# The gates' columns on the first v pair, four-tile o slots, and the rows' chain spread over the last group, in a hybrid mLSTM/conv decoder layer

## The reference, cut to what matters

```python
h_in = rms_norm(x, pre_mix_norm_w)
proj = h_in @ w_in            # q, k (1024) | v (512) | o (512) | gates (8) | conv value (512) | conv gate (512)
qk = silu(causal_depthwise_conv(qk_raw, qk_conv_w) + qk_conv_b)          # width 4
gates = gates + gate_bias; i_pre, f_pre = gates[:, :4], gates[:, 4:]
h = mlstm_chunkwise(q, k, v, i_pre, f_pre)    # chunks of 128; per chunk and head: cumulative log
                                              # forget gate, running maximum, decays, carried state
y_mlstm = sigmoid(o_pre) * layer_norm(h) * w
u = conv_val * sigmoid(conv_gate); u = causal_depthwise_conv(u, conv_w)  # width 31
y_conv = silu(layer_norm(u))
x = x + rms_norm(concat(y_mlstm, y_conv) @ w_out)
x = x + rms_norm(square(relu(rms_norm(x) @ w_ff1)) @ w_ff2)
```

## Time and profile before

| | us |
|---|---|
| three runs | 2145.79, 2147.93, 2150.26; median 2147.93 |
| the profiled execution | 2149.32 |
| its span | 2147.5 |
| TensorE busy | 2090.3 |
| VectorE busy | 1441.8 |
| ScalarE busy | 903.3 |
| GpSimd busy | 416.3 |

### The profile page before, as it was taken

The page is one execution under the profiler, slowest core; times in us unless marked ns, Lnnn a source line. Parts: engine busy times, 40 slices in busy tenths (PEclk is TensorE's granted clock), DMA queues, the critical chain, the costliest instruction groups (busy, mean ns, idle before and its releaser), DMA issues. The chain is left out here.

```text
span 2147.5 us, 27070 instructions
## 1 busy us (share of the span) xinstructions
PE 2090.3 (97%) x10177; PEld 1752.4 (82%) x10177; DVE 1441.8 (67%) x1965; ACT 903.3 (42%) x1512; POOL 416.3 (19%) x254
## 2 busy tenths in 40 slices
PE   7999999999979999999999999999999999999998
PEld 5897878888978888778888778888888888888886
DVE  6797999889157777776666866666654536534276
ACT  5532434234344544655544644455423313313153
POOL 0000000000010231243332332233172144400012
PEclk9999999999999999999999999999999999999999
DMA  5021212112174686664455655544875454443375
GB/s 198 25 89 47 67 40 84 55 40 81 55 271 154 223 270 222 210 199 141 139 159 181 227 161 162 162 147 125 280 253 222 142 230 172 175 176 138 137 253 207
DMA packets 253520, 339.18 MB, mean 158 GB/s; under 512 B 11536, under 2 KB 196112, under 8 KB 239568
## 3 DMA queue, kind: packets, MB, share of 16 engines
q1 hardware_dynamic: 219344, 316.29, 43.9%
q10 hardware_dynamic: 33728, 21.04, 3.1%
q0 software_dynamic: 320, 0.13, 0.0%
HBM read 226.14 MB, written 111.28 MB: 157 GB/s over the span
## 5 line engine op out<-in xcount | busy, mean ns | idle before, releaser
L1651 PE MATMUL psum<-x_hi,w_hi_P 128*128 128x512 f32 x896 | 351.6, 392 | 13.1 <-DVE x_lo L1595 8.9
L1855 PE MATMUL psum<-w_hi,hid_hi 128*128 128x512 f32 x896 | 349.3, 390 | 1.9 <-DVE hid_lo L1745 1.9
L1651 PE MATMUL psum<-x_hi,w_lo_P 128*128 128x512 f32 x896 | 350.4, 391 | 0.0
L1651 PE MATMUL psum<-x_lo,w_hi_P 128*128 128x512 f32 x896 | 350.2, 391 | 0.0
L1855 PE MATMUL psum<-w_lo,hid_hi 128*128 128x512 f32 x896 | 349.1, 390 | 0.0
L1855 PE MATMUL psum<-w_hi,hid_lo 128*128 128x512 f32 x896 | 349.1, 390 | 0.0
L1745 DVE TENSOR_TENSOR hid_lo<-hid_raw,hid_hi 128x1024 fp32r<-128x1024 f32 x112 | 182.1, 1663 | 202.4 <-ACT hid_hi L1740 202.4
L1564 POOL TENSOR_TENSOR w_raw<-w_raw 128x512 f32<-128x512 f32 x128 | 179.7, 1427 | 409.6 <-DVE w_lo_P L1577 391.6
L1740 ACT ACTIVATE hid_hi<-hid_raw 128x1024 fp32r<-128x1024 f32 x112 | 112.9, 1051 | 341.5 <-DMA hid_raw<-scratch_hid 341.5
L1577 DVE TENSOR_TENSOR w_lo_P<-w_raw,w_hi_P 128x512 fp32r<-128x512 f32 x224 | 182.4, 826 | 109.1 <-ACT w_hi_P L1573 106.0
L1573 ACT ACTIVATE w_hi_P<-w_raw 128x512 fp32r<-128x512 f32 x224 | 136.7, 627 | 255.0 <-PE psum L1651 254.8
(11 more groups left out here) (241 smaller groups left out, 3895.4 us busy)
## 6 DMA issues: line engine op xcount, KB each, us to landing
scratch_hid<-stage SPq DMA_DIRECT2D x224, 256.0 KB, 3.7
hid_raw<-scratch_hid SPq DMA_DIRECT2D x56, 1024.0 KB, 4.9
w_raw<-in_w SPq DMA_DIRECT2D x52, 1024.0 KB, 5.1
w_grain<-in_w SPq DMA_DIRECT2D x48, 512.0 KB, 4.9
x_raw<-scratch_h2s SPq DMA_DIRECT2D x14, 1024.0 KB, 7.5
w_raw<-in_w_in SPq DMA_DIRECT2D x25, 512.0 KB, 3.6
scratch_h2s<-h2s SPq DMA_DIRECT2D x8, 1280.0 KB, 9.2
scratch_qk<-qout ACTq DMA_DIRECT2D x16, 512.0 KB, 3.1
```

Of the source, the lines that this page charges most:

```text
L1651: mm = nc.tensor.matmul(psum[:, bank_1(op, g), :], l, r, start=kt == 0 and i == 0, stop=kt == 3 and i == 2)
L1855: mm = nc.tensor.matmul(psum[:, bank, :], l, r, start=f == 0 and k == 0, stop=f == NFP - 1 and k == 2)
```

## The change

- The slots of the gates are gone. The eight gate columns stand beside the two tiles of the first v pair: 264 columns for each of the two chunks of a slot, each in a PSUM bank of its own (`with_gates`, `banks_of`). The pair's weights are loaded in two halves by kt, and the first slot waits for the second half only before kt 4. ScalarE copies the gate columns to a small buffer `gates_c`, and TensorE transposes it after slot 73; the stores and loads through HBM are gone.
- Chunks 0 to 5 of o keep their slots of two tiles by two chunks (six slots); chunks 6 to 15 have one slot each (`ow`), all four tiles by one chunk: 24 products 512 columns wide. `N_SLOTS` is 96 (100 before). The last group's slots from 70 on take four banks in turn; banks 4 and 5 are for the rows.
- The rows' chain goes to indices of group 3 and after (`ROWS_SLOT` = 72): TensorE after slots 73 (transposes of the gates), 76, 78, 79, 81; ScalarE at 74, 78, 80; VectorE at the end of its indices 76 (`forget_rows`), 78 (`carry_rows`), 80 (`floor_rows`), 82 (`column_rows`).
- The last unit's norm steps stand at 1 and 2 indices after its last tap.
- The output weights are split in pairs at indices 91 to 94 on both engines, and loaded from slot 87's end. Chunk 0's exponentials stand on ScalarE at index 94, ahead of the last evacuation. TensorE makes chunk 0's scores (in banks 4 and 5) before it waits for the last evacuations.

The diff, cut (without the index arithmetic and the splitting of functions into parts):

```diff
-         + [("gates", 0, tb) for tb in range(NTB)] + pair_slots("o", 0) + pair_slots("o", 1))
+         + [("o", pair, m) for pair in range(2) for m in range(O_PAIRS)] + [("ow", 0, c) for c in range(2 * O_PAIRS, NCH)])
...
-RING = [0, 1, 2, 3] + [0, 1] + [2, 3, 0, 1] + [2, 3, 0, 1] + [2, 3] + [0, 1, 2, 3] + [0] + [2, 3] + [0, 1]
+RING = [0, 1, 2, 3] + [0, 1] + [2, 3, 0, 1] + [2, 3, 0, 1] + [2, 3] + [0, 1, 2, 3] + [0, 1, 2, 3]
+GATE_COLS = 2 * H
+VG = 2 * P + GATE_COLS
+VG_TILES = [TILES.index(("v", 0)), TILES.index(("v", 1))]
+W_IN_TILES = [t for t in range(N_TILES) if t not in VG_TILES]
...
+ROWS_SLOT = SLOTS.index(("qk", 6, 0))
+def banks_of(s):
+    if s >= ROWS_SLOT - 2:
+        return [(s - ROWS_SLOT + 2) % 4]
+    at = s + sum(with_gates(slot) for slot in SLOTS[:s])
+    return [(at + k) % 6 for k in range(2 if with_gates(SLOTS[s]) else 1)]
...
+LAST_UNIT_AT = {AT_MEAN: 1, AT_CENTER: 1, AT_SQUARE: 1, AT_VAR: 2, AT_RSTD: 2, AT_NORM: 2, AT_SILU: 2}
...
+WO_SPLITS = {N_SLOTS - 5: (0, 1), N_SLOTS - 4: (2, 3), N_SLOTS - 3: (4, 5), N_SLOTS - 2: (6, 7)}
...
+        w_cols = KT * GATE_COLS + W_RING * KT * P
+        w_hi_all = sb("w_hi", [P, w_cols], F32R)
+        gates = keep["gates"] = sb("gates_c", [P, 2, H, NCH])
+        sb("pad_w", [P, PAD_W])
+        with nc.sbuf_tensor("w_raw", [P, w_cols], F32) as w_raw_all:
             pass
-        w_lo = sb("w_lo", [P, W_RING, KT, P], F32R)
+        w_lo_all = sb("w_lo", [P, w_cols], F32R)
...
+                first = tile[0] if with_gates(SLOTS[s]) else tile[-1]
+                pe.wait_ge(sem["w_hi"], first + 1)
+                pe.wait_ge(sem["w_lo"], first + 1)
+                for bank in banks:
+                    before = last_in_bank(s, bank)
+                    if before is not None:
+                        by = "dve" if SLOTS[before][0] == "val" else "act"
+                        pe.wait_ge(sem["evac"][by], evacs(before, by))
...
+                if with_gates(SLOTS[s]):
+                    for k in range(2):
+                        o = psum[:, banks[k], 0:VG]
+                        for kt in range(KT):
+                            if k == 0 and kt == KT // 2:
+                                pe.wait_ge(sem["w_hi"], tile[1] + 1)
+                                pe.wait_ge(sem["w_lo"], tile[1] + 1)
+                            hi, lo = tokens(h_hi, kt, (2 * tb + k) * P, P), tokens(h_lo, kt, (2 * tb + k) * P, P)
+                            pairs = [(hi, vg_hi[:, kt]), (hi, vg_lo[:, kt]), (lo, vg_hi[:, kt])]
...
+                elif kind == "ow":
+                    o = out.rearrange("p (a b) -> p a b", a=W_RING)
+                    for kt in range(KT):
+                        hi, lo = tokens(h_hi, kt, tb * P, P), tokens(h_lo, kt, tb * P, P)
+                        pairs = [(hi, w_hi[:, :, kt, :]), (hi, w_lo[:, :, kt, :]), (lo, w_hi[:, :, kt, :])]
...
-                if s == TAIL_SLOT + 1:
-                    pe.wait_ge(sem["c_rstd"], 2 * N_UNITS)
+                if s == ROWS_SLOT + 1:
+                    pe.wait_ge(sem["evac"]["act"], evacs(ROWS_SLOT - 1, "act"))
+                    tail["gates"](pe)
+                if s == ROWS_SLOT + 4:
                     tail["carry_in"](pe)
-                if s == TAIL_SLOT + 2:
+                if s == ROWS_SLOT + 6:
                     tail["carry_out"](pe)
-                if s == TAIL_SLOT + 3:
+                if s == ROWS_SLOT + 7:
+                    tail["carry_decay"](pe)
+                if s == ROWS_SLOT + 9:
                     tail["columns"](pe)
...
+                    both = psum[:, banks[0]:banks[0] + 2, :]
+                    nc.scalar.activation(gates[:, :, :, 2 * tb:2 * tb + 2].rearrange("p g h c -> p c (g h)"),
+                                         both[:, :, 2 * P:VG], ACT.Copy)
+                    ps, to = both[:, :, 0:2 * P], to.rearrange("p (c d) -> p c d", c=2)
...
-                if s == TAIL_SLOT:
+                if s == ROWS_SLOT + 2:
                     nc.scalar.preload_act_table_set(LN_EXP)
                     tail["softplus"](act)
                     nc.scalar.preload_act_table_set(SILU_TANH)
-                if s == TAIL_SLOT + 1:
+                if s == ROWS_SLOT + 6:
+                    nc.scalar.preload_act_table_set(LN_EXP)
...
-                if s >= N_SLOTS - 3:
-                    if s == N_SLOTS - 1:
-                        nc.scalar.preload_act_table_set(LN_EXP)
-                        tail["weights"](act, 0)
-                    for kt in {N_SLOTS - 3: range(4), N_SLOTS - 2: range(4, 7), N_SLOTS - 1: ()}[s]:
-                        tail["split_wo"](act, kt)
+                for kt in WO_SPLITS.get(s, ()):
+                    tail["split_wo"](act, kt)
+                if s == N_SLOTS - 2:
+                    nc.scalar.preload_act_table_set(LN_EXP)
+                    tail["weights"](act, 0)
+                    nc.scalar.preload_act_table_set(SILU_TANH)
+                if s == N_SLOTS - 1:
+                    nc.scalar.preload_act_table_set(LN_EXP)
 
...
-            tail["rows"](dve)
-            tail["wo_low"](dve, range(KT - 1))
+                if s == ROWS_SLOT + 4:
+                    tail["forget_rows"](dve)
+                if s == ROWS_SLOT + 6:
+                    tail["carry_rows"](dve)
+                if s == ROWS_SLOT + 8:
+                    tail["floor_rows"](dve)
+                if s == ROWS_SLOT + 10:
+                    tail["column_rows"](dve)
+                tail["wo_low"](dve, WO_SPLITS.get(s, ()))
             tail["exponents"](dve)
...
+            nc.scalar.activation(gi[:], psum[0:NG, 4, 0:P], ACT.Identity, bias=gate_bias[:, 0:1]).then_inc(sem["gi"], 1)
+            link(nc.scalar.activation(gf[:], psum[0:NG, 4, P:2 * P], ACT.Identity, bias=gate_bias[:, 1:2]), 1)
...
+        def gates_t(pe):
+            pe.wait_ge(sem["ident"], 4)
+            for g in range(2):
+                mm = nc.tensor.transpose(psum[0:NG, 4, g * P:(g + 1) * P],
+                                         keep["gates"][:, g].rearrange("p h c -> p (h c)"), ident[:])
+            mm.then_inc(sem["gates_t"], 1)
...
+            pe.wait_ge(sem["cols_done"], 2)
+            scores(0)
             for e in ("act", "dve"):
                 pe.wait_ge(sem["evac"][e], evacs(N_SLOTS - 1, e))
-            pe.wait_ge(sem["cols_done"], 2)
-            scores(0)
...
-            split_wo(act, KT - 1)
...
```

More of the change, by code:

```diff
@@ L79, in tiles_of, with with_gates, o_slot @@
     kind, n, _ = slot
+    if kind == "ow":
+        return [TILES.index(("o", k)) for k in range(W_RING)]
     return [TILES.index(t) for t in ([(kind, 2 * n), (kind, 2 * n + 1)] if kind in ("v", "o") else [(kind, n)])]
+def with_gates(slot):
+    return slot[:2] == ("v", 0)
+def o_slot(c):
+    return SLOTS.index(("o", 1, c // 2) if c < 2 * O_PAIRS else ("ow", 0, c))
 def first_use(tile):
@@ L184, in th_uses @@
 def th_uses(s):
-    return sum(k in ("gate", "gates", "v", "o") for k, _, _ in SLOTS[: s + 1])
+    return sum(k in ("gate", "v", "o", "ow") for k, _, _ in SLOTS[: s + 1])
 def th_stores(s, parity):
@@ L192, in th_stores @@
     for i in range(s + 1):
-        k = SLOTS[i][0]
-        if k in ("gates", "v", "o") and (th_uses(i) - 1) % 2 == parity:
-            n += 2 if k == "gates" else 1
+        if SLOTS[i][0] in ("v", "o", "ow") and (th_uses(i) - 1) % 2 == parity:
+            n += 1
     return n
@@ L202, in last_th_user @@
     for i in range(s):
-        if SLOTS[i][0] in ("gate", "gates", "v", "o") and th_uses(i) - 1 == n - 2:
+        if SLOTS[i][0] in ("gate", "v", "o", "ow") and th_uses(i) - 1 == n - 2:
             return i
@@ L322, in slot @@
                 tile = tiles_of(SLOTS[s])
[L323 to L329, removed]
-                r = RING[tile[0]]
-                if kind in ("v", "o"):
+                banks = banks_of(s)
+                out = psum[:, banks[0], :]
@@ L415, in evacuate @@
                     return
-                ps = psum[:, s % BANKS_A, :]
+                banks = banks_of(s)
+                ps = psum[:, banks[0], :]
                 act.wait_ge(sem["proj"], s + 1)
@@ L799, in load_w_out @@
         def load_w_out(sp):
-            sp.wait_ge(sem["proj"], SLOTS.index(("o", 1, NCH // 4 - 1)) + 1)
+            sp.wait_ge(sem["proj"], o_slot(NCH // 2 - 1) + 1)
             for kt in range(KT):
@@ L1395, in vector @@
             weigh(0)
-            wo_low(dve, (KT - 1,))
             yc_low(0)
@@ L1431, in phase_b @@
         return {"sync": sync, "gpsimd": gpsimd, "tensor": tensor, "scalar": scalar, "vector": vector,
-                "tail": {"parameters": load_parameters, "w_out": load_w_out, "masks": make_masks, "load_gates": load_gates, "store_rows": store_rows,
-                         "softplus": softplus, "carry_in": carry_in, "carry_out": carry_out, "columns": columns,
-                         "exps": exps, "rows": rows, "split_wo": split_wo, "wo_low": wo_low, "exponents": exponents_0,
```

(11 more changed lines are left out.)

147 lines of the change are left out of this document (80 added, 67 removed).

## The result

The changed kernel takes 2152.11 us in the median of 20 runs, the kernel before 2148.97 in 20 runs beside it. The ratio is 1.0014, 95% interval 1.0008 to 1.0021: 3.1 us slower (1.7 to 4.5), within 0.2%. The profiled execution of after took 2149.75 us (span 2147.9), that of before 2149.32 (span 2147.5).

A forecast was written before the change was run, and what follows sets the result against it. TensorE, at 97% of the span, was taken as the bound. Input projection -5.2, passage to chunk 0's numerators +1.4 and clock loss +5.8 us gave +2.0 on 2147.9: 2149.9 us, range 2143.0 to 2155.5.

The forecast's parts named there:

- The slots: Input projection on TensorE: four gate slots gone, 21.8 us off; ten wide o slots, 3.1 us off.
- The v pair: First v slots: 1.3 us on for 8 more columns, 1.5 us back from a shorter weight wait; -0.2 us taken.
- rival of slow 264 columns: In the first v slots, products 264 columns wide fall off the fast rate: +123 us at most, 2273; chance 0.02.
- Wait 1: After slot 76 TensorE stands for a_max, behind VectorE's convolution and row operations, from 476.4 to 487.7: 11.3 us.
- the walk: Link-by-link timing of ScalarE, VectorE and TensorE around the rows' chain, in the earlier profile's clock; gave stands of 11.3, 7.0, 3.0 us.
- rival that the rows are ahead of TensorE: At the rows' chain TensorE never waits: 2122.8 us, or about 2135 if partly so; chance 0.1.
- rival of a table load that costs twice its record: Four ScalarE table loads, two before a_max and two before chunk 0's numerators, add 5.1 us: 2155.0; chance 0.02.
- Waits 2 and 3: TensorE stands 7.0 us for m_in after slot 78, and 3.0 us before the columns after slot 81.
- TensorE at the end of the phase: End of the input projection: slot savings and new stands sum to -5.2 us, before any clock loss.
- The hand-over: From slot 95's end to chunk 0's numerators: 6.2 us against 4.8, +1.4 us, with ScalarE's exponentials ahead of the last evacuation.
- The clock at the hand-over: After a 4.6 us stand behind chunk 0's scores, its numerators may run at half clock: 0 to 1.7 us, 0.9 taken.
- The late clock: Half clock lasts 6.1 us after the three row stands, losing 3.05 each, and 1.7 before chunk 0's numerators: 2155.0; chance 0.18.

The follow-up runs named there:

- the run without waits: Changed kernel with TensorE's a_max visit after slot 79, m_in and decay after 84, columns after 88, other engines' parts moved along: 2126.85 us, ratio 0.9888 to the kernel before.

## Why the prediction was right, point by point

**The slots.** Wide o slots took 5.45 us (24 products from 610.22 to 615.67), as taken from the 512-wide slots; the run without waits bears out the four gates' slots (26.4 us at the end of slot 95 where 26.5 were taken). Right.

**The v pair, a term mis-sized.** -0.2 us was predicted, -1.0 measured. The gap before the first tile's second part was 0.52 us where before stood 1.84, so 1.3 came back of the 1.5 expected. But 8 more columns cost little: the 372 products behind that gap took (161.71 - 116.67)/372 = 0.1211 us each against (163.45 - 117.30)/384 = 0.1202 before, 0.35 us in all where the slope between 256 and 512 columns gave 1.3. Timeline of TensorE, the first v slot of after:

```profile
116.03 0.28 PE L392 MATMUL psum<-w_hi,big_lo 128*128 128x264 f32 x1
116.67 0.36 PE L392 MATMUL psum<-w_hi,big_hi 128*128 128x264 f32 x1 [0.36 <-DVE w_lo L689]
```

The rival of slow 264 columns falls with it.

**Wait 1.** 11.3 us predicted, 10.7 to the row products (10.51 and the 0.2 around them). The timelines of ScalarE and of VectorE in after, in the order of the walk:

```profile
465.58 1.28 ACT L624 ACT_TABLE_LOAD   x1
466.88 0.36 ACT L922 ACTIVATE gi<-psum,gate_bias 64x128 f32<-64x128 f32 x1
...
468.54 1.28 ACT L626 ACT_TABLE_LOAD   x1
469.83 2.01 ACT L484 ACTIVATE w_hi<-w_raw 128x1024 fp32r<-128x1024 f32 x2
...
478.41 1.15 ACT L552 ACTIVATE qout<-qraw,par_a 128x1024 f32<-128x1024 f32 x1 [3.35 <-DMA scratch_qk<-qout]
```

```profile
479.59 3.93 DVE L733 SCALAR_TENSOR_TENSOR qout<-qraw,par_a,qout 128x1024 f32<-128x1024 f32 x3 [2.29 <-ACT qout L552]
...
485.08 0.42 DVE L992 TENSOR_TENSOR_SCAN a_max<-ones,gi 64x128 f32<-64x128 f32 x1
```

Every link is there: softplus with its two table loads, the two weight splits, the first tap, the convolution, the rows. TensorE was 1.7 us ahead by then, so the walk's 481.6 for the convolution is 479.9 here, and it came at 479.59. The rival that the rows are ahead of TensorE falls. An activation starts 0.02 us after the table load before it ends (466.88), so the rival of a table load that costs twice its record falls too; by "ScalarE: Activation LUTs", What ACT_TABLE_LOAD costs, in the Trainium skill, a drain of 1.38 us would have stood there, and the trace does not agree.

**Waits 2 and 3.** 7.0 and 3.0 predicted, 6.8 and 3.3 measured. The last links were those named: m_last, and the exponentials (floor, L969).

**TensorE at the end of the phase.** -5.2 + 4.9 for the clock = -0.3 predicted, -0.3 measured. Misses cancel in it: 0.8 us too little taken off for the v pair and 0.5 too much put on for the waits, against 1.0 too little for the clock. The terms as measured give -0.6, so 0.3 us is not accounted for, and that the sum met the number is in part luck. After waits 1 and 2 the loss was 2.2 and 2.1 us (2.2 each predicted), but after wait 3, of 3.13 us, it was 1.6, where 0.5 had been taken from a range of 0 to 1.7.

**The hand-over.** 6.2 predicted, 6.29 measured, with ScalarE idle before the exponentials (1.26) and wk last. Right.

**The clock at the hand-over: the number by luck.** 0.9 us was taken, from 0 to 1.7. The granted clock stayed at 0.50 from 622 to 626, through numerators and state update of chunk 0: numerators to y transposes took 633.39 - 621.96 = 11.4 us against 630.60 - 621.55 = 9.1 before, 2.4 us. The range ended at 1.7, which is the numerators' share; the 8 products of the state update behind them were not in it. But from there to chunk 2's scores after took 647.20 - 633.39 = 13.8 us and before 645.87 - 630.60 = 15.3. Before had half clock there too, for all its work from 634.75 to 640.9; in after chunk 1's numerators began only at 637.54, and the clock was back at 640.4. So 1.5 us came back, 0.9 is left, and the term is right by a cancellation that the prediction does not have. At chunk 2's scores the sum of the forecast, +2.0, stands at +2.1.

**What failed: nothing changes behind the hand-over.** The prediction had "no reason" for a change there, and took from the earlier trace rows that the clock stays up after 2.3 us of idle time. Behind the 2.30 us before chunk 9's y transposes it fell in after and held in before, 1.7 us; behind the 2.5 us of the MLP it held in after and fell in before, 1.5 us the other way. The work and the waits are the same in both. Whether the 1.1 us between the forecast's 2.0 and the medians' 3.1 come from this stays open; they lie inside the interval.

**The late clock** (7.1, chance 0.18) was not it, but not far off: the half clock lasted 4.6 us after waits 1 and 2, just over the 4.5 us at which that rival decides, and 3.4 after wait 3. The clock's losses up to chunk 2's scores are 2.2 + 2.1 + 1.6 + 0.9 = 6.8 us, between the 5.8 of the forecast and its 10.9, and inside the bounds given (3.4 to 9.6).

## What to carry to other kernels

Before a consumer is put at "slot s" of an in-order engine, read from the trace when the producer's own work with index s ends: here VectorE ended its work with index 76 some 7 us after TensorE had ended slot 76, unseen because nothing waited for it, and 27 us taken off TensorE's list turned into waits of 21 us and 6 us of lost clock. Moving the consumers a few slots later, or the producer one slot earlier, gave most of the saving back (24 and 22 us less than before). A stand of 2 to 3 us on TensorE has to be priced with a clock that may fall or not: shorten it, or fill it with products nobody reads (2.8 us by the traces at the hand-over). And before the rest of a difference is put down to the change, follow both traces past it to a place where the code is the same: here two falls of the clock, one in each kernel, were worth 1.7 and 1.5 us, as much as half of the result.

## What the runs showed that was not expected

- The length of a stand did not decide alone whether the clock fell. Behind 2.30 to 2.32 us at chunk 9 it held in six kernels and fell in three; behind 2.34 us it held; behind 2.5 us in the MLP it held in after and fell in before; behind 3.00 us before the numerators it fell in one kernel (0.77 us at 619.57) and held in another (0.46 at 594.63). Behind waits 1 to 3 (10.5, 6.6 and 3.13 us) and the 3.10 us of the run with the producer earlier it fell. What told equal stands apart stays open.
- The clock need not fall while TensorE stands: after wait 3 it was granted 1.00 in 530:531, and fell only once the products had begun again; after the 3.10 us wait of the kernel with the earlier rows it fell only in 480:481, more than 1 us into the work (0.86). Behind 3.02 us at wait 3 of the run with unread products it fell during the stand (0.72 in 527:528). The loss comes all the same, behind the wait, where it is easily put down to something else.
- 264 columns cost 0.9 ns more than 256, not the 3.3 ns of the slope between 256 and 512.
